# A weight split moved ahead of VectorE's wait for the matmuls of a recurrence round

## What is computed

```python
def hgrn2_mixer(u, w_in, w_out, lb, o_gain):
    q, z_f, v, g = jnp.split(u @ w_in, [...], axis=-1)      # four products of 1024 x 1024
    q = jax.nn.silu(q)
    f = lbf + (1 - lbf) * jax.nn.sigmoid(z_f)
    log_f = jnp.log(jnp.maximum(f, MIN_FORGET))
    k = (1 - lbf) * (1 - sig)
    ...
    b = jnp.cumsum(lfc, axis=1)                             # decay between two tokens: exp(b_t - b_s)
    attn = jnp.einsum('bhtd,btshd,bshd->bhts', qc, decay, kc)
    o = einsum(attn, vc) + einsum(qc * exp(b), state)
    ...
    o = o * rsqrt(mean(o * o) + eps) * o_gain * silu(g)
    return o @ w_out
```

## Time and profile before

| | |
|---|---|
| time, median of 3 runs | 1719.53 us (1717.67 to 1721.64) |
| the profiled execution: its own time | 1722.02 us |
| the profiled execution: span | 1719.9 us |
| TensorE matmuls busy | 1592.9 us, 93% of the span |
| VectorE, ScalarE, GpSimd busy | 654.3, 580.8, 26.9 us |
| mean granted TensorE clock | 0.943 |

### The profile page before, as it was taken

How to read it: one execution, slowest core, us unless ns; L and a number is a source line. 1 busy time by engine, 2 the same in 40 slices (tenths; PEclk the granted TensorE clock), 3 DMA queues, 4 the chain that set the end, 5 groups by cost and what they waited for, 6 DMA issues and landing times.

```text
span 1719.9 us, 27757 instructions
## 1 busy us (share of the span) xinstructions
PE 1592.9 (93%) x11990; PEld 1300.0 (76%) x11990; DVE 654.3 (38%) x1121; ACT 580.8 (34%) x912; POOL 26.9 (2%) x45
## 2 busy tenths in 40 slices
PE   7898979999999988999998999988899999999997
PEld 4887868999998965899998868888655655555563
DVE  3645755333335534554454444653211110111110
ACT  2531224333334444444444546443111111111111
POOL 1000000000000000000000000001000000000000
PEclk8898989999998989999997979999799999999999
DMA  9564833888876620455552323626499999999996
GB/s 331 165 217 148 256 111 117 290 286 289 294 250 216 216 79 23 146 193 181 187 176 73 121 74 123 245 74 184 164 395 394 393 394 395 394 393 395 395 392 234
DMA packets 261656, 404.23 MB, mean 235 GB/s; under 512 B 5013, under 2 KB 172210, under 8 KB 261554
## 3 DMA queue, kind: packets, MB, share of 16 engines
q1 hardware_dynamic: 259520, 397.43, 66.3%
q0 software_dynamic: 1648, 5.18, 1.0%
q10 hardware_dynamic: 386, 0.11, 0.0%
HBM read 401.63 MB, written 1.07 MB: 234 GB/s over the span
## 4 chain that ended last, share of the span: by engine, by line
PE 87%; DVE 8%; ACT 3%; issue 1%; DMA 1%; SPq 0%; ACTq 0%; DVEq 0%
PE ps L1691 31%; PE ps L2138 13%; PE ps L1874 7%; PE ps L2160 7%; PE ps L1704 5%; PE ps L2125 4%; PE ps L2170 3%; PE ps L1731 3%; PE ps L1747 2%; PE ps L1811 2%; PE ps L1901 2%; PE ps L1715 1%; DVE wsplit L1091 1%; DVE sq L1137 1%; PE ps L1912 1%
## 5 line engine op out<-in xcount | busy, mean ns | idle before, releaser
L1691 PE MATMUL ps<-u,wsplit 128*128 128x256 f32 x4440 | 567.1, 290 | 26.7 <-DVE u L1144 19.4
L1691 PEld LDWEIGHTS ps<-u,wsplit 128*128 128x128 f32 x4440 | 555.9, 197 | 33.6 <-issue 27.1
L1091 DVE TENSOR_TENSOR wsplit<-arena,wsplit 128x1024 fp32r<-128x1024 f32 x258 | 313.1, 1223 | 358.7 <-ACT wsplit L708 352.4
L708 ACT ACTIVATE wsplit<-arena 128x1024 fp32r<-128x1024 f32 x258 | 269.7, 1056 | 304.2 <-PE ps L1691 137.6
L2138 PE MATMUL ps<-arena 128*64 128x256 f32 x1408 | 157.4, 382 | 0.8 <-DVE arena L1610 0.8
L1615 DVE TENSOR_TENSOR arena<-arena,ps 128x256 f32<-128x256 f32 x32 | 13.5, 421 | 368.5 <-ACT arena L1057 368.5
L2138 PEld LDWEIGHTS ps<-arena 128*64 128x64 f32 x1408 | 101.7, 138 | 61.7 <-issue 13.5
L1874 PE MATMUL ps<-hid,wsplit 128*128 128x256 f32 x1056 | 130.2, 283 | 0.0
L1874 PEld LDWEIGHTS ps<-hid,wsplit 128*128 128x128 f32 x1056 | 128.2, 192 | 0.0
L1704 PE MATMUL ps<-wsplit,u 128*128 128x256 f32 x672 | 87.4, 293 | 9.1 <-DVE wsplit L1091 9.1
L1704 PEld LDWEIGHTS ps<-wsplit,u 128*128 128x128 f32 x672 | 85.4, 201 | 10.4 <-DVE wsplit L1091 9.3
(11 more groups left out here) (325 smaller groups left out, 1332.5 us busy)
## 6 DMA issues: line engine op xcount, KB each, us to landing
arena<-in_w SPq DMA_DIRECT2D x66, 2048.0 KB, 19.3
late<-in_w SPq DMA_DIRECT2D x30, 2048.0 KB, 19.5
arena<-in_mod_w SPq DMA_DIRECT2D x48, 1024.0 KB, 7.9
arena<-in_ffn_w_in SPq DMA_DIRECT2D x44, 1024.0 KB, 5.9
arena<-in_ffn_w_out SPq DMA_DIRECT2D x22, 1024.0 KB, 5.7
arena<-in_a_w_in SPq DMA_DIRECT2D x16, 1024.0 KB, 6.4
arena<-in_kv_mod_w SPq DMA_DIRECT2D x8, 1024.0 KB, 7.1
arena<-in_kv_w SPq DMA_DIRECT2D x8, 1024.0 KB, 8.0
```

The lines of the kernel that those rows point to most:

```text
L708: act.activation(piece_buf(p, 0), piece_src(p), ACT.Copy).then_inc(hi_done, 1)
L1091: dve.tensor_tensor(piece_buf(p, 1), piece_src(p), piece_buf(p, 0).bitcast(F32), ALU.subtract).then_inc(lo_done, 1)
L1691: mm = pe.matmul(o, w_[:, k, :], u[:, x_, k, :], start=first, stop=last)
```

## The change

One line in VectorE's loop. After `select(r)` and ahead of `decayed(r + 1)`, VectorE splits up to the first piece of round r + 1 plus 3, that is piece 21 + 2r: the second piece of round r + 2 (for r = 6 piece 33, the second piece of the output projection's first pair). There it stands seven times, r = 0 to 6. The next turn then finds that piece done and has one piece left to split.

```diff
@@ -1260,6 +1260,7 @@
                     lo_upto(p["w"] + LOOKAHEAD)
                 select(r)
                 if r < 7:
+                    lo_upto(jobs[("v" if r + 1 < 4 else "g") + str(r + 1)][0]["w"] + LOOKAHEAD)
                     decayed(r + 1)
                     if r + 1 < 7:
                         products(r + 1)
```

## The result

The changed kernel takes 1705.05 us (median of 4 runs, 1702.82 to 1707.52) against 1720.59 us (median of 4, 1717.67 to 1722.09) for the kernel before: ratio 0.9922, 95% interval 0.9908 to 0.9936, that is 13.4 us less (11.0 to 15.8); the two medians lie 15.5 us apart, which is inside that interval. The profiled execution took 1702.86 us with a span of 1700.7 and a mean granted clock of 0.949.

What follows compares the result with a forecast made beforehand. TensorE, busy 93%, was taken as the bound, stalled by VectorE's split standing behind decay operations. Terms 13.3 + 0.7 + 1.15 = 15.2 us, off the median 1719.5, gave 1704.3 us; range 1700.5 to 1709.

Steps and rivals of the forecast that it cites:

- The first term: Rounds 2 and 3: both take what round 1 takes, stalls and slow clock gone, 13.3 us less.
- the stalls' 9.1 us alone: Rounds 2 and 3: rival that stalls go but slow products stay, 1708.6 us in all; chance 0.06.
- The second term: Rounds 4 to 7: with the split early each takes 12.65 us, 0.7 us less (bounds 0 and 0.9).
- The third term: End of the recurrence: one of two splits ahead of select(7) leaves the path, 1.15 us less.
- The cover: VectorE's wait for TensorE: moved split done 8.5 us ahead in round 1, some 2.9 us slack per later round.
- The slower rival: All 7 rounds: a late ScalarE high part delays the moved split and decayed behind it, 1723 us; chance 0.04.
- The loads: SP can issue loads earlier, which takes a wait from ScalarE; counted as 0.
- The rival that loads become the bound: Rounds with g pieces: loads land 3 us too late on up to 3 rounds, 1713 us; chance 0.06.
- What may come on top: L1832 behind round 7: shorter gap may keep the clock up, up to 1.7 us more; counted 0, chance 0.18.
- That I pass all on: Stages after the recurrence, up to 700 us and experts from 1240 us: the whole gain survives, nothing deducted.
- a stage after 250 us that has grown: Changed profile, behind the recurrence: a listed sign that the prediction is wrong; no size given.

Runs made afterwards that it cites:

- only_v: Kernel before, with the split moved only in the turns of rounds 0 and 1 (pieces 21 and 23): ratio 0.9927 to the kernel before.
- filler: Kernel before, no split moved, 16 idle matmuls on TensorE ahead of the v products of rounds 2 and 3: ratio 0.9981 to the kernel before.
- extra3: Changed kernel plus 3 extra VectorE operations behind each moved split: 96.4 us from round 0's own products to L1832, as in the changed kernel.
- extra8: Changed kernel plus 8 extra VectorE operations behind each moved split: 111.9 us from round 0's own products to L1832, against the changed kernel's 96.4.
- late_hi: Changed kernel, ScalarE's wait for the round's dense product put ahead of its two high parts: 96.4 us from round 0's own products to L1832.
- only_end: Kernel before, with the split moved only in the turn of round 6 (piece 33): profiled span 1712.5 us against 1719.9.
- warm_end: Changed kernel plus 14 idle matmuls on TensorE right behind round 7, ahead of L1832: ratio 0.9896 to the kernel before.

## Why the prediction was right

The forecast was 1704.3 us (15.2 less than 1719.5); measured are 1705.05, 13.4 us less by the ratio and 15.5 by the two medians.

- **The first term, 13.3 us:** `only_v` has 13.35. That the whole difference of the rounds is won, and not the stalls' 9.1 us alone, was the choice in it, and `filler` shows the other part by itself: 3.84 us.
- **The second term, 0.7 us:** 0.84. I had taken 12.65 us for a round; the first g round is at 12.69 and the next at 12.60.
- **The third term, 1.15 us:** the gap shrank by 1.14.
- **The cover:** the first moved split waited 2.15 us for ScalarE and had 8.48 us left, against 8.5 forecast; later turns had 2.96 against 2.9. `extra3` and `extra8` confirm it from either side. The slower rival's condition was not reached: in `late_hi` a high part 5 us later cost nothing.
- **The loads:** I had ScalarE's wait of 8.47 us gone; it has shrunk to one of 1.86 us, and TensorE is idle in no round. The rival that loads become the bound did not happen; `only_v` does not show a delay either.
- **What may come on top:** this term, taken as 0 with only a gain beside it in the range, was wrong in sign. I expected the shorter gap either to keep the clock up or to change nothing. It did neither: the part of B behind the gap became 1.7 us longer. The step that failed is the sentence "if the clock then falls a little later instead, that is given back": it allows for no loss, while the low clock reached past the one group (L1832) on through the output products.
- **That I pass all on:** the sum survives, but not because the later stages are blind to the change. The prediction's own sign of being wrong, "a stage after 250 us that has grown", did show: the rest of B took 2.4 us more. And C is 3.7 us shorter (1404.9 against 1408.6), by the entry to the experts, which the kernel before does in 44.6 us at clock 0.89 and the changed one in 40.5 at 1.00:

```profile
1220.10:1264.70 44.60, 41.06 (x295) 26.68 (x295) 5.03 (x14) 5.40 (x9) 0.00 (x0) 0.89 0.69 254
```

```profile
1204.90:1245.40 40.50, 36.99 (x294) 23.80 (x294) 4.98 (x14) 5.40 (x9) 0.00 (x0) 1.00 0.76 279
```

In the twelve profiles the two go together: the five with 64.7 us in the rest of B have 40.5 or 40.6 at the entry and the lowest C (1404.5 to 1405.0), the seven others have 62.3 to 63.6, 42.0 to 44.6 and 1406.9 to 1409.5. `only_end`, which moves piece 33 alone, has both, so they come with that move, as far as one profile of each kernel can tell. By what path, over more than 900 us, is open. That the gain here nearly equals the losses in B, and the time so came out near the sum, is luck.

So A is settled by experiments (the parts add up to 0.03 us). Of B's 4.1 us more, 1.7 lie in the part behind the gap, whose slow clock went when the gap was filled; the other 2.4, and the 3.7 by which C is shorter, come with the move of piece 33 by a path that is open.

## What to carry to other kernels

When an in-order engine feeds two consumers, look at what it does while it waits: a piece of work whose input is already there, standing behind a wait that it does not need, can cost the other engine its own length and that of everything between; here 1.15 us of work stood behind 4.8 us of decay operations, TensorE had 1.5 us of other work to cover them, and the stall of some 4.6 us came twice, which with the clock behind it was 13 us. Price such a stall with the slow matmuls behind it (3.84 of 13.35 us here), and check the cover in the engine that takes the work (3 us per turn here, gone with 5.76 us more). And when a gap on TensorE gets shorter without closing, read the granted clock of the stage behind it before counting the gain: shortening the gap by 1.14 us made the matmuls behind it 1.7 us slower, and filling it with idle matmuls won 3.5 us there.

## What I had not expected of the hardware

A shorter idle gap was followed by a longer stretch at the lower clock. In the kernel before, with 5.11 us idle, the clock was at 0.60 over the next 4.2 us and at 1.00 after that; in the changed one, with 3.97 us idle, it was at 0.51 over 8.3 us. The rows of the kernel before:

```profile
221.30:225.50 4.20, 3.58 (x16) 3.41 (x16) 1.77 (x3) 1.08 (x2) 0.00 (x0) 0.60 0.68 224
225.50:231.00 5.50, 5.33 (x32) 4.93 (x33) 0.00 (x0) 1.90 (x4) 0.00 (x0) 1.00 0.01 3
```

More profiles show the same: read in windows of 0.2 us, the low stretch ended 3.0 to 4.0 us behind the start of the products in the five kernels with a gap of 5.11 or 8.51 us, and 7.6 to 9.6 us behind it in the five with 3.97 or 2.83 us left unfilled. The two groups overlap in time (the products start at 208.1 us in `only_v`, with the long gap, and at 206.1 and 214.1 in `extra3` and `only_end`, with the short one), which speaks against their place in the program's time as the cause. By these rows the cost of a gap does not grow evenly with its length; why, they don't show.

The Trainium skill, "TensorE: Matmul & The Clock Gate", section "HAM oscillation — how this bites in real kernels", treats waits between bursts of matmuls as the cause of slow bursts. The runs here agree: with the wait filled, the products behind it took 6.00 us in place of 7.62 (`filler`) and 2.02 in place of 3.75 (`warm_end`).

The first 110 us, which the change does not touch, move every span by up to 6 us: round 0's own products start between 103.8 and 109.8 us. In the profile of the kernel before the sums of the first norm take 6.97 us, in that of the changed kernel 5.50 us, for the same 32 matmul records (timelines of PE, before, then changed). The clock is 0.50 from 30.2 us on in the one, from 35.8 us on in the other:

```profile
36.95 6.97 PE L1747 MATMUL ps<-ones,sq 128*128 128x1 f32 x32
```

```profile
34.20 5.50 PE L1748 MATMUL ps<-ones,sq 128*128 128x1 f32 x32
```

The four runs of the changed kernel lie at 1702.82, 1702.86, 1707.23 and 1707.52 us. `extra3` and `late_hi`, with the same A and a start at 109.8, have spans of 1705.3 and 1704.6 against 1700.7 with a start at 105.4; that the runs' two levels are these two starts is likely, not shown, since a run without a profile has no such rows. A comparison of two single profiles of this kernel can be off by this much: of the 19.2 us between the two spans here, 4.4 lie ahead of 110 us.
